# Expert weights in a three-block transformer kernel: 16 KB runs and 2 MB transfers in place of 8 KB and 1 MB, and the last up products column half by column half

## The reference, cut to what matters

```python
def expert_choice_ffn(xn, w_router, w_gate, w_up, w_down):
    cap = CAPACITY_FACTOR * S // N_EXPERTS          # 64 tokens for each of 16 experts
    aff = softmax(xn @ w_router)
    top_aff, top_idx = lax.top_k(swapaxes(aff, 1, 2), cap)
    xg = xn[bidx, top_idx]
    hid = silu(einsum('becd,edf->becf', xg, w_gate)) * einsum('becd,edf->becf', xg, w_up)
    y = einsum('becf,efd->becd', hid, w_down) * top_aff[..., None]
    return zeros((B, S, D)).at[bidx, top_idx].add(y)
```

## Time and profile before

| | us |
|---|---|
| median of 3 runs | 2094.88 |
| the profiled execution: its time | 2095.13 |
| the profiled execution: its span | 2093.0 |

### The profile page before, as it was taken

The page is one execution under the profiler, slowest core; times in us unless marked ns, Lnnn a source line. Parts: engine busy times, 40 slices in busy tenths (PEclk is TensorE's granted clock), DMA queues, the critical chain, the costliest instruction groups (busy, mean ns, idle before and its releaser), DMA issues.

```text
span 2093.0 us, 23655 instructions
## 1 busy us (share of the span) xinstructions
PE 2052.3 (98%) x9752; PEld 1382.8 (66%) x9752; DVE 987.8 (47%) x1457; ACT 547.2 (26%) x1078; POOL 29.6 (1%) x16
## 2 busy tenths in 40 slices
PE   9999999999999999999999999999999999999998
PEld 5677565776888877786678788878754443333357
DVE  3776544556655454674476667644541101101145
ACT  4745452320001232203222435330140000000024
POOL 0121000000000000000000000000000000000000
PEclk9999999999999999999999999999999999999999
DMA  8311111322222120223221211212659999999961
GB/s 211 81 41 59 63 41 41 81 101 78 83 81 91 46 81 25 81 81 68 85 81 41 81 41 41 75 58 81 241 189 397 414 408 421 420 419 419 420 247 41
DMA packets 117978, 316.79 MB, mean 151 GB/s; under 512 B 38064, under 2 KB 46384, under 8 KB 93680
## 3 DMA queue, kind: packets, MB, share of 16 engines
q1 hardware_dynamic: 115520, 313.28, 40.3%
q10 hardware_dynamic: 2352, 2.00, 0.4%
HBM read 312.83 MB, written 2.10 MB: 150 GB/s over the span
## 4 chain that ended last, share of the span: by engine, by line
PE 88%; DVE 4%; ACT 4%; issue 2%; DMA 1%; DVEq 0%; SPq 0%; ACTq 0%
PE bank L459 37%; PE bank L473 17%; PE bank L3038 10%; PE bank L3088 5%; PE bank L2952 2%; PE bank L2974 2%; PE bank L1830 2%; PE bank L1406 1%; PE bank L1428 1%; PE bank L1456 1%; PE bank L2543 1%; DMA wide<-in_w_exp_gate 1%; PE bank L2533 1%; PE bank L2966 1%; PE bank L2958 1%
## 5 line engine op out<-in xcount | busy, mean ns | idle before, releaser
L459 PE MATMUL bank<-hT,ring 128*128 128x256 f32 x1168 | 268.7, 384 | 1.6 <-DVE gq L742 1.0
L459 PEld LDWEIGHTS bank<-hT,ring 128*128 128x128 f32 x1168 | 221.5, 192 | 37.8 <-issue 5.8
L473 PE MATMUL bank<-hT,ring 128*128 128x512 f32 (+1 forms) x416 | 187.8, 603 | 4.8 <-DMA ring<-in_l_w_in 4.8
L459 PE MATMUL bank<-l_quarter,l_quarter 128*128 128x256 f32 x672 | 155.2, 383 | 3.1 <-DVE gq L1750 2.6
L459 PEld LDWEIGHTS bank<-l_quarter,l_quarter 128*128 128x128 f32 x672 | 126.8, 191 | 23.5 <-DVE gq L1750 3.0
L473 PEld LDWEIGHTS bank<-hT,ring 128*128 128x128 f32 (+1 forms) x416 | 77.0, 190 | 96.9 <-issue 91.2
L3038 PE MATMUL bank<-wide,xg 128*64 128x512 f32 x488 | 124.7, 595 | 0.8 <-DMA wide<-in_w_exp_gate 0.8
L3038 PE MATMUL bank<-ring,xg 128*64 128x512 f32 x352 | 100.2, 594 | 0.0
L3206 DVE TENSOR_TENSOR xT<-bank,xT 128x512 f32<-128x512 f32 x32 | 22.1, 692 | 155.8 <-PE bank L2952 155.7
L3038 PEld LDWEIGHTS bank<-wide,xg 128*64 128x64 f32 x488 | 38.8, 137 | 75.0 <-issue 75.0
L459 PE MATMUL bank<-ring,hT 128*128 128x256 f32 x384 | 86.7, 381 | 0.2 <-DVE gv_hi L742 0.2
(11 more groups left out here) (573 smaller groups left out, 3354.4 us busy)
## 6 DMA issues: line engine op xcount, KB each, us to landing
wide<-in_w_exp_down SPq DMA_DIRECT2D x38, 1024.0 KB, 12.6
ring<-in_l_w_in SPq DMA_DIRECT2D x18, 2048.0 KB, 7.9
wide<-in_w_exp_gate SPq DMA_DIRECT2D x34, 1024.0 KB, 10.1
wide<-in_w_exp_up SPq DMA_DIRECT2D x27, 1024.0 KB, 12.2
ring<-in_w_exp_up SPq DMA_DIRECT2D x25, 1024.0 KB, 9.4
ring<-in_w_exp_down SPq DMA_DIRECT2D x21, 1024.0 KB, 13.7
ring<-in_w_in SPq DMA_DIRECT2D x10, 2048.0 KB, 8.2
ring<-in_w_exp_gate SPq DMA_DIRECT2D x19, 1024.0 KB, 10.9
```

Source lines behind the costliest of these rows:

```text
L459: mm = pe.matmul(self.out(n)[:, half * 256:half * 256 + 256], *halves[half][k], start=i == 0 and not job["goes_on"], stop=False, skip_grou ...
L473: mm = pe.matmul(self.out(n), *mats[i], start=i == 0, stop=i == len(mats) - 1)
```

## The change

**Blocks and transfers.** A block is still 1 MB, but a partition now holds half of a run of 4 neighbouring rows (16 KB), and the order is half by half, in each half the two blocks of the first expert and then the two of the second. Two blocks that stand next to each other in this order are the two halves of such runs, and where they go into a place of 2 MB they come in one transfer. `last_tile` becomes 24 p + i//4*4 + i%2*2 + i//2%2 + 1: the blocks are used in the order 0, 2, 1, 3 of each four. Before the first step of a half TensorE waits for the blocks 0 and 2 of it, that is for both transfers where they are of 2 MB.

**Places.** There are now five places of 2 MB (1, 3, 5, 7 and 13; the last one is that of the embedding's weights and the place 0, joined) and the single places 0, 9 to 12, 14, 15 and 16. A unit of two blocks takes a 2 MB place or two single ones; singles that have no fitting partner are dropped from the list. Place 9 may be used up to block 25 instead of 31.

**Up products.** In the second up half the order of the loops turns: first the four steps `k` of the column half 0, then those of the column half 1. A semaphore `up_half` is raised after the first column half, and VectorE's first multiplication into `hid` waits for it in place of the whole product.

**Row order.** `even_first` and `in_order` become the order of four rows.

```diff
-                for q in range(4):
+                for half in range(2):
                     for e in range(2):
-                        stream.append((a[w][0, 2 * p + e, q * 256:(q + 1) * 256, :].rearrange("(p k) n -> p k n", k=2), 2, D))
-                        blocks.append(len(stream) - 1)
+                        four = a[w][0, 2 * p + e, half * 512:(half + 1) * 512, :].rearrange("(p k) n -> p k n", k=4)
+                        for q in range(2):
+                            stream.append((four[:, 2 * q:2 * q + 2, :], 2, D))
+                            blocks.append(len(stream) - 1)
+                            four_rows[len(stream) - 1] = four
...
-        LIMIT = {9: NB + 8, 10: NB, 11: 3 * NB, 12: NB, 15: 1, 16: 16}
+        LIMIT = {LATER: NB + 8, 9: NB + 2, 10: NB, 11: 3 * NB, 12: NB, 15: 1, 16: 16}
+        FIRST = [(15, TOPMOST), (1,), (3,), (5,), (LATER, 9), (7,), (10, 11), (12, 16)]
...
-        waiting = [(n, None) for n in (15, TOPMOST, *range(EMB), 16)]
-        for e in range(NB * len(EXP)):
-            n, by = waiting.pop(0)
-            while e >= LIMIT.get(n, e + 1):
-                n, by = waiting.pop(0)
...
+        waiting = []
+
+        def single_after(e, i):
+            return next((n for n, x in enumerate(waiting) if n >= i and x[0] in singles and e < LIMIT.get(x[0], e + 1)), None)
+
+        for u in range(NB * len(EXP) // 2):
+            e = 2 * u
+            if u < len(FIRST):
+                places = [(n, None) for n in FIRST[u]]
+            else:
+                while waiting[0][0] in singles and (single_after(e + 1, 0) != 0 or single_after(e + 1, 1) is None):
+                    waiting.pop(0)
+                places = [waiting.pop(0)]
+                if places[0][0] in singles:
+                    places.append(waiting.pop(single_after(e + 1, 0)))
...
-                last_tile[EXP[p][i]] = t0 + 24 * p + i + 1
-        for i in range(2):
-            place_free[i] = (tiles_done, last_tile[WBG[1]])
-        for i in range(3, 7):
-            place_free[i] = (l1_final, GATED + 6)
-        for i in range(4):
-            place_free[7 + i] = (tiles_done, last_tile[WO2[i // 2]])
...
+                last_tile[EXP[p][i]] = t0 + 24 * p + i // 4 * 4 + i % 2 * 2 + i // 2 % 2 + 1
+        place_free[0] = (tiles_done, last_tile[WBG[1]])
+        place_free[2] = (l1_final, GATED + 6)
+        place_free[6] = (tiles_done, last_tile[WO2[0]])
+        place_free[8] = (tiles_done, last_tile[WO2[1]])
+        place_free[14] = (sums_t, 1)
...
         def even_first(x):
-            return x.rearrange("p (q r f) -> p q f r", q=2, r=2)
+            return x.rearrange("p (r f) -> p f r", r=4)
...
+                            apart = which == 1 and half == 1
+                            ks = range(4 * half, 4 * half + 4)
+                            for k, ns in [(k, (n,)) for n in range(2) for k in ks] if apart else [(k, range(2)) for k in ks]:
+                                pair = [EXP[p][8 * which + 4 * half + 2 * e + k // 2 % 2] for e in range(2)]
+                                if k % 2 == 0 and 0 in ns:
                                     for j in pair:
                                         wait_block(pe, j)
-                                for n in range(2):
+                                for n in ns:
...
+                                if apart and ns == (0,) and k == KD - 1:
+                                    mm.then_inc(up_half, 1)
...
-                        dve.wait_ge(tiles_done, base + 16)
+                        if n == 0:
+                            dve.wait_ge(up_half, up_before + p + 1)
+                        else:
+                            dve.wait_ge(tiles_done, base + 16)
```

More of the change, by code:

```diff
@@ L290, in rows @@
             return parts
[L291 to L298, removed]
-        topmost = nc.alloc_sbuf_tensor_at("topmost", [P, 2, D], F32, offset=top)
@@ L302, in build, with four_at @@
[L302 to L306, removed]
-        LIMIT = {9: NB + 8, 10: NB, 11: 3 * NB, 12: NB, 15: 1, 16: 16}
+        def four_at(x):
+            return x, [[x[:, 2 * q + k, :] for k in range(2)] for q in range(2)]
@@ new lines, in build @@
+        early = [rows(at(f"wide{i}", 4 * i, [P, 2, D])) for i in range(2)]
+        fours = {n: four_at(x) for n, x in (
+            (1, at("wide_a", 8, [P, 4, D])[:, :, :]), (3, at("wide_b", 16, [P, 4, D])[:, :, :]),
+            (5, ring[WO2[0] % RING][:, 0:4 * D].rearrange("p (k n) -> p k n", k=4)),
+            (7, ring[WO2[1] % RING][:, 0:4 * D].rearrange("p (k n) -> p k n", k=4)),
+            (13, at("wide_c", 0, [P, 4, D])[:, :, :]))}
+        topmost = nc.alloc_sbuf_tensor_at("topmost", [P, 2, D], F32, offset=top)
@@ new lines, in build @@
+        EMB, TOPMOST, LATER = 13, 14, 0
+        singles = {LATER: early[1], 9: rows(at("once0", 44, [P, 2, D])),
+                   10: [at("once1", 50, [P, D])[:, :], at("once1", 54, [P, D])[:, :]],
+                   11: rows(at("once2", 36, [P, 2, D])), 12: rows(at("once3", 32, [P, 2, D])), TOPMOST: rows(topmost),
+                   15: [at(f"first{t}", t, [P, D])[:, :] for t in (48, 52)],
+                   16: [at(f"first{t}", t, [P, D])[:, :] for t in (56, 58)]}
+        LIMIT = {LATER: NB + 8, 9: NB + 2, 10: NB, 11: 3 * NB, 12: NB, 15: 1, 16: 16}
@@ L308, in build @@
+        FIRST = [(15, TOPMOST), (1,), (3,), (5,), (LATER, 9), (7,), (10, 11), (12, 16)]
+        EMB_TO = NB + 5
         ple_w_loaded = sem("ple_w_loaded")
         wpg_loaded = [sem(f"wpg_loaded{i}") for i in range(2)]
-        wide_at = {WPL: places[EMB]}
+        wide_at = {WPL: early[0]}
         load_sem = {WPL: (ple_w_loaded, 32)}
-        taken_from, last_place, times_of = {}, {}, {}
+        taken_from, last_of, whole_at = {}, {}, {}
+        level_of = {n: 16 if n < 5 or n >= TOPMOST else 32 if n < 9 else 96 if n == 9 else 64 for n in (*fours, *singles)}
@@ new lines, in single_after @@
+        def single_after(e, i):
[10 more added lines that the diff above has]
+                    places.append(waiting.pop(single_after(e + 1, 0)))
+            if places[0][0] in fours:
+                n, by = places[0]
+                whole, halves = fours[n]
+                order.append(E0 + e)
+                level_of[n] += 16
+                for q in range(2):
+                    wide_at[E0 + e + q] = halves[q]
+                    load_sem[E0 + e + q] = (landed[n], level_of[n])
+                whole_at[E0 + e] = (whole, four_rows[E0 + e])
+                taken_from[E0 + e] = by
+                last_of[n] = E0 + e + 1
+                waiting.append((n, E0 + e + 1))
+            else:
+                for q, (n, by) in enumerate(places):
+                    j = E0 + e + q
+                    order.append(j)
+                    wide_at[j] = singles[n]
+                    whole = whole_of.get(id(singles[n]))
+                    if whole is not None:
+                        whole_at[j] = (whole, stream[j][0])
+                    level_of[n] += 16 if whole is not None else 32
+                    load_sem[j] = (landed[n], level_of[n])
+                    taken_from[j] = by
+                    last_of[n] = j
+                    waiting.append((n, j))
+            if e <= EMB_TO < e + 2:
@@ L396, in issue_blocks @@
                     sp.wait_ge(*place_free[by])
+                    sp.wait_ge(tiles_done, last_tile[last_of[LATER]])
                 else:
                     sp.wait_ge(tiles_done, last_tile[by])
-                if whole_at.get(j) is not None:
-                    sp.dma_start(whole_at[j], src).then_inc(load_sem[j][0], 16)
+                if j in whole_at:
+                    sp.dma_start(*whole_at[j]).then_inc(load_sem[j][0], 16)
                 else:
@@ L3081, in tensor @@
                         for k, ns in [(k, (n,)) for n in range(2) for k in ks] if apart else [(k, range(2)) for k in ks]:
-                            pair = EXP[p][16 + k // 2 * 2:18 + k // 2 * 2]
+                            pair = [EXP[p][16 + 4 * half + 2 * e + k // 2 % 2] for e in range(2)]
                             if k % 2 == 0 and 0 in ns:
```

26 lines of the change are left out of this document (5 added, 21 removed).

## The result

The changed kernel takes **2102.76 us** (median of 5 runs, 2101.78 to 2103.26) against 2094.88 us (also of 5 runs, 2093.45 to 2095.03): a ratio of 1.0039, with a 95% interval of 1.0025 to 1.0052. It is 7.9 us slower, a small difference, but the interval leaves out 1. Forecast were 2103.0 us and slower. The profiled execution took 2101.78 us with a span of 2099.7 us.

What follows compares the result with a forecast made beforehand. DMA and TensorE were taken to run level, with no DMA reserve at the end; block 175's 10.3 - 5.0 + 1.3 - 2.0, plus 3.5 for whole-half waits, gave +8.1 us, forecast 2103.0 us, range 2097 to 2108.

Steps and rivals of the forecast that it cites:

- what bounds the stage: Experts' stage: DMA (59.9 us a pair) and TensorE (59.3) run level; the reserve is used up at block 175 in pair 7.
- The +3.5 after it: After block 175: waiting for both transfers of a half makes what follows longer by 3.5 us.
- the hole: First refill: block 17 goes out at count 9, 1574.97 instead of 1564.67 us, making the later stream 10.3 us late.
- the 5.0 of rest: Between 1577 and 1740 us: a queue that is behind no longer rests, giving back 5.0 us.
- what becomes of the delay: Later stream: of the 10.3 us delay, 5.0 us of rest is given back and 1.3 added for fewer places.
- the rate: DMA with 16 KB runs: 422 GB/s instead of 420, 0.5% more, worth -2.0 us (ends -4.8 and +4.0).
- rival 2: The DMA rate rises by 1.2 to 2.5%, giving 2097.5 to 2101 us; chance 0.17.
- the rests: Queue with five 2 MB places: rests of 1.3 us near 1720 to 1730 and in pairs 4 and 5's first up halves.
- the hid step: Pairs 2 to 6: TensorE gains 0.9 us each, worth 0 on the path because it waits longer for transfers.
- where the waits stand: TensorE's waits for weights: 10 to 14 us instead of 0.8, mostly in pairs 6 and 7, each ahead of a half.
- the order of the rows and of the loops: Scattered rows_tm writes before the stage and second up half's loops: taken as 0, rows uncertain by some 4 us either way.
- rival 1: Transfers' fixed cost was the limit and 2 MB transfers halve it, so TensorE is the bound: 2089.7 us; chance 0.07.

Runs made afterwards that it cites:

- half_waits: The kernel before, with TensorE waiting ahead of each half for all four of its blocks instead of two ahead of each quarter: 2097.86 us, ratio 1.0019.
- early_refill: The changed kernel, with the list of places reordered after the 16 first blocks so that three 2 MB places come first: 2100.15 us, ratio 1.0025 to the kernel before.
- two_of_1mb: The changed kernel, with each unit brought in two 1 MB transfers with 8 KB runs to the same place: 2104.01 us, ratio 1.0040 to the kernel before.
- up_half_alone: The kernel before, with only the hid part of the change (loop order of the second up half, up_half semaphore): 2095.53 us, ratio 1.0004.
- no_up_half: The changed kernel, with the old up loop order and both multiplications into hid waiting for the whole product: 2106.56 us, ratio 1.0056 to the kernel before.
- ten_places: The kernel before, with the place topmost given up after block 72, leaving 10 places of 1 MB: 2096.72 us, ratio 1.0012.

## Why the prediction was right, and where it wasn't

**Right: what bounds the stage.** DMA and TensorE run level, and block 175 with what follows it sets the end. It landed at 418.8 us from the start of pair 0, for 413.8 before; the sum said 4.6 us later, measured are 5.0. The +3.5 after it is right as well: from there to the end of the stage the changed kernel takes 50.3 us for 47.1, 3.2 more, and half_waits alone costs 3.2.

**Right: the hole.** Its place (unit 8, `LATER`, count 9), its 10.3 us of later issue, and the 5.0 of rest that it takes back in the kernel before. *Wrong: that this holds in the changed kernel.* There early_refill gives 2.2 to 2.6 and not 5.3, though it takes only part of the hole away. The step that failed is "what becomes of the delay": it took the two numbers of the kernel before and added 1.3 for fewer places, as if the three were independent. They aren't: with fewer places the queue reaches its limit sooner, and then the hole is forgotten and the limit counts.

**Mis-sized: the rate.** Forecast 0.5%, upper end 1.2%; measured 426 for 420, 1.4%. The line through 2 KB and 8 KB runs put the fixed time of a run at 3 ns, and the busy shares at 7. From 8 to 16 KB it is more: at 16 engines 420 GB/s is 312 ns for 8 KB and 426 is 615 ns for 16 KB, so 303 ns for the second 8 KB and 9 ns fixed. As the sum counts it, that would be -5.5 us instead of -2.0. But it is not worth that: two_of_1mb shows 0.7 at block 175 and some 1.4 in the time, not told from 2.0.

So the condition of rival 2, a rate higher by 1.2 to 2.5%, came true, and its time, 2097.5 to 2101, did not: it took for granted that a higher rate moves the landing. (By the sum itself its 2.5% would give some 2095, not 2097.5.)

**Mis-sized the other way: the rests.** +1.3 was forecast. From 1577 to 1971 the changed kernel moves 419 to 420 GB/s, at a rate of 426 without rest: 163 x 7 / 426 + 231 x 6 / 426 = 5.9 us of rests. It is 4.6 too few, beside the 3.5 us too few for the rate. These two errors have one origin and nearly cancel: a faster queue fills its five places sooner and then rests. two_of_1mb shows it: at 420 GB/s in the same places it moves 419 and 418 in the two stretches and rests 163 x 1 / 420 + 231 x 2 / 420 = 1.5 us, near the 1.3 that the prediction had for its 422. With the measured sizes the sum gives 10.3 - 5.0 + 5.9 - 5.5 = 5.7 us later for block 175, where 5.0 is measured; 0.7 stays unexplained. That the total was right to 0.3 us is luck; the terms were not.

**Wrong: the hid step is worth 0.** It is in the kernel before (up_half_alone) and isn't in the changed one (3.6 to 3.8 us, no_up_half). The prediction argued that TensorE only reaches its waits earlier. It overlooked that TensorE also releases the places earlier, and that a queue short of places moves with them.

**Half right: where the waits stand.** "10 to 14 us, mostly in pairs 6 and 7": 12.7 us, of which 7.2 in the pairs 6 and 7. But the other 5.5 stand in the pairs 3 to 5, where the prediction had only some rest and no waits, and make them longer by 1.6, 0.9 and 0.9. In each of them the chain passes through the second transfer of the first up half. Its place comes free at the end of the first gate half (chain: 1733.11), other units are ahead of it in the queue, it lands 13.1 us later, and TensorE has only the second gate half and two combines (7.0 + 2 x 1.9 = 10.8 us) to do in between. Before, with eleven places for blocks that are used two in a quarter, there were four quarters between a block's release and the use of its follower, some 20 us (59.3 / 12 x 4, an estimate).

**Right: the order of the rows and of the loops costs nothing.** The groups, to set beside the earlier trace rows:

```profile
L3293 DVE TENSOR_TENSOR hid<-bank,pos 128x512 f32<-128x512 f32 x16 | 17.1, 1066 | 100.1 <-PE bank L3068 100.1
...
L3163 ACT ACTIVATE rows_tm<-bank,ffn_rc 128x512 f32<-128x512 f32 x8 | 7.5, 1130 | 0.0
```

1066 ns for 1059 and 1130 for 1142. The groups show this for the order of the rows. The loops show in the chain: the second up half of pair 2 takes TensorE 7.07 us before and after.

**The fixed cost of a transfer.** Transfers of 1 MB and of 2 MB, both with runs of 8 KB, move the same 420 GB/s in a queue kept full, so rival 1, in which larger transfers free TensorE of the bound, did not happen. The Trainium skill (DMA: Bandwidth & Descriptors, section "Anatomy of one DMA — SWDGE (gpsimd) path") gives 2 us plus bytes over 436 GB/s for each DMA, by a fit for transfers issued from GpSimd. In this full queue of SyncE's a block of 1 MB takes 2.50 us and not the 4.4 of that fit, an estimate from the page, so these runs don't agree with it. Nor would the fit's own price have made TensorE the bound, as the prediction says: twelve transfers at 6.8 us are 82 us a pair, above TensorE's 59.3. Only the ratio of 6.8 to 8.8, applied to the measured 59.9 us, would.

**What stays open.** The single prices in the kernel before (5.1 for the hole, 3.2 for whole-half waits, 2.0 for the lost MB) add up to 10.3, and without the rate and the hid step the changed kernel would be at about +13 (11.8 and 1.4), if these two simply add, which this study gives reason to doubt. How the difference divides among them was not tried.

## What to carry to other kernels

When a queue of prefetches and an engine run level, ask for each load how long before its use its place comes free: larger units are released later and needed earlier, and cost twice. A plan's first wait behind an in-order queue is worth walking through; here one single place in a list held up six blocks whose places came free before it. And don't add up terms that share a limit: a gain in rate, a hole and a faster consumer were each worth one thing with eleven places and another with five.

## What the runs showed of the hardware

**The length of a run counts up to 16 KB.** 408 GB/s with 2 KB runs (one stretch of 3 us), 420 with 8 KB, 426 with 16 KB, with the queue kept full; with 8 KB runs the size of the transfer made no difference (420 and 419 GB/s with 1 MB, 420 with 2 MB).

**A wait can cost its length and a half clock after it.** In half_waits TensorE waits 3.3 us for a transfer at the end of pair 6; the next half takes 8.61 us instead of 7.09, and the stretch after the wait has a granted clock of 0.55, mostly the lower of the two levels, 1.2 GHz. First its chain (start us, us, what), then the stretch (columns as in the earlier trace rows):

```profile
1946.97 13.40 DMA ring<-in_w_exp_gate
1960.51 8.61 PE bank L3038 x32
```

```profile
1960.50:1964.00 3.50, 3.49 (x10) 1.25 (x12) 0.00 (x0) 0.00 (x0) 0.00 (x0) 0.55 1.03 426
```

The same stands in ten_places after a wait of 2.4 us (granted clock 0.67 in the 3.5 us behind it), in early_refill after one of 2.7 (0.69) and in two_of_1mb after one of 2.9 (0.69), but not in the changed kernel after two of 2.7 (1.00), nor in no_up_half after one of 2.4 (1.00). So the length of the wait alone doesn't tell. In early_refill and two_of_1mb it cost nothing at the end, since TensorE waited for the next transfer again.
